# Order of quarter products and turned tiles where a row norm hands over to the next matrix product

## The reference

```python
# block 1
x = x + rmsnorm(merged @ w_out[l], norm_mix_post[l])
h = rmsnorm(x, norm_ffn_pre[l])
f = jnp.square(jax.nn.relu(h @ w_ff1[l])) @ w_ff2[l]
x = x + rmsnorm(f, norm_ffn_post[l])
# block 2
h = jnp.einsum('bsd,de->bse', x, w_in[l])
...
x = layernorm_2(DEEPNORM_ALPHA * x + mix, ln1_g[l], ln1_b[l])
hid = jax.nn.silu(x @ w_gate) * (x @ w_up)
x = layernorm_2(DEEPNORM_ALPHA * x + hid @ w_down, ln2_g[l], ln2_b[l])
# block 3
h = x @ w_in[l]
...
x = layer_norm(DEEPNORM_ALPHA_3 * x + mix, ln1_g[l], ln1_b[l])
xa = memory_cross_attention(x, mem, ...)          # begins with x @ xa_wq
x = layer_norm(DEEPNORM_ALPHA_3 * x + xa, ln2_g[l], ln2_b[l])
ff = hierarchical_moe(x, ...)
```

## Time and profile before

| what | value |
|---|---|
| median of 3 runs | 3252.77 us (3252.38 to 3253.66) |
| the profiled execution's own time | 3252.19 us |
| its span, first to last instruction | 3250.5 us |
| TensorE matmul busy | 3020.5 us, 93% of the span |
| VectorE / ScalarE / GpSimd busy | 1443.4 / 694.7 / 123.4 us (44% / 21% / 4%) |
| mean granted TensorE clock | 0.958 of full |
| last part of the span | from about 2700 us on the experts' weights stream in at some 424 GB/s with all DMA engines busy |

### The profile page before, as it was taken

How to read it: one execution, slowest core, us unless ns; L and a number is a source line. 1 busy time by engine, 2 the same in 40 slices (tenths; PEclk the granted TensorE clock), 3 DMA queues, 4 the chain that set the end, 5 groups by cost and what they waited for, 6 DMA issues and landing times. The chain is left out here.

```text
span 3250.5 us, 38522 instructions
## 1 busy us (share of the span) xinstructions
PE 3020.5 (93%) x15046; PEld 2156.2 (66%) x15046; DVE 1443.4 (44%) x2554; ACT 694.7 (21%) x1596; POOL 123.4 (4%) x147
## 2 busy tenths in 40 slices
PE   8979998999999889988999999999889977999997
PEld 4468766888868668887688886877756634333332
DVE  3454424334353667457543354424744232333335
ACT  0321113220010543471101001114531212111111
POOL 1000000000000200000100000000100001000000
PEclk9989999999999979998999999998999988999998
DMA  9121212222221102201223222222012208999995
GB/s 379 53 78 52 78 58 78 78 104 85 78 80 65 40 27 78 78 1 39 78 78 104 78 89 92 78 81 79 2 66 78 67 0 337 423 425 422 424 424 218
DMA packets 129894, 420.48 MB, mean 129 GB/s; under 512 B 6705, under 2 KB 35778, under 8 KB 108242
## 3 DMA queue, kind: packets, MB, share of 16 engines
q1 hardware_dynamic: 121842, 379.48, 30.6%
q10 hardware_dynamic: 3024, 23.59, 1.8%
q0 software_dynamic: 4880, 15.35, 1.3%
HBM read 394.81 MB, written 23.59 MB: 129 GB/s over the span
## 5 line engine op out<-in xcount | busy, mean ns | idle before, releaser
L777 PE MATMUL bank<-arena 128*128 128x256 f32 x5152 | 1127.7, 382 | 30.5 <-issue 15.5
L777 PEld LDWEIGHTS bank<-arena 128*128 128x128 f32 x5152 | 985.7, 192 | 173.1 <-issue 23.1
L1073 PE MATMUL bank<-arena 128*128 128x256 f32 x1652 | 362.7, 382 | 10.0 <-PEq L131 3.5
L1073 PEld LDWEIGHTS bank<-arena 128*128 128x128 f32 x1652 | 316.5, 192 | 54.9 <-issue 11.3
L178 PE MATMUL bank<-arena 128*128 128x512 f32 (+8 forms) x676 | 230.0, 495 | 33.1 <-PEq L3463 11.5
L178 PEld LDWEIGHTS bank<-arena 128*128 128x128 f32 (+2 forms) x676 | 120.0, 196 | 137.5 <-issue 120.3
L425 PE MATMUL bank<-arena 128*128 128x512 f32 x384 | 167.7, 598 | 4.2 <-PEq L1685 2.0
L3903 DVE TENSOR_TENSOR arena<-arena,bank 128x512 f32<-128x512 f32 x128 | 87.8, 688 | 139.0 <-PE bank L3807 136.7
L841 DVE TENSOR_TENSOR arena<-arena 128x1024 f32<-128x1024 f32 x46 | 56.3, 1223 | 182.9 <-PE bank L777 179.5
L425 PEld LDWEIGHTS bank<-arena 128*128 128x128 f32 x384 | 73.1, 191 | 95.5 <-issue 95.5
L3807 PE MATMUL bank<-arena 128*128 128x512 f32 x256 | 123.1, 615 | 4.4 <-DVE arena L3889 4.4
(11 more groups left out here) (561 smaller groups left out, 3523.9 us busy)
## 6 DMA issues: line engine op xcount, KB each, us to landing
arena<-in_moe_w_gate_dram SPq DMA_DIRECT2D x64, 1024.0 KB, 20.4
arena<-in_moe_w_up_dram SPq DMA_DIRECT2D x64, 1024.0 KB, 18.7
arena<-in_moe_w_down_dram SPq DMA_DIRECT2D x32, 2048.0 KB, 24.1
arena<-in_w_in_dram SPq DMA_DIRECT2D x29, 2048.0 KB, 7.9
arena<-in_w_ff_dram SPq DMA_DIRECT2D x16, 2048.0 KB, 7.9
x_slots<-arena ACTq DMA_DIRECT2D x8, 2048.0 KB, 33.6
arena<-in_w_out_dram SPq DMA_DIRECT2D x8, 2048.0 KB, 7.8
arena<-in_w_gate_dram SPq DMA_DIRECT2D x11, 1024.0 KB, 5.4
```

What stands on the lines that cost most here:

```text
L777: last = pe.matmul(bank[:, m, :], lhsT, rhs, start=fresh and m == 0 and k == 0, stop=k == 3, skip_group_check=True)
L1073: last = pe.matmul(bank[:, m, :], x[:, k, m * P:(m + 1) * P], w[:, k, :], start=opening and m == 0 and k == 0, stop=k == w.shape[1] - 1, s ...
```

## The change

It does four things.

- **Order on TensorE.** After product 1 of step 0, only tile 2 is turned; then comes product 2 of step 0; then tile 3 is turned; then come products 1 and 2 of step 1, and then products 5, 6, 7, 3, 4 of step 0, the same five of step 1, and the later steps as before.
- **Room for it.** Products 1 and 2 of step 1 get bank 4 (`of_12_ahead`), and the copy of its product 1 gets the first 512 columns of `spare` (`first_ahead`).
- **Copies of turned tiles.** In the layer norms ScalarE makes both copies of tiles 0 and 1, at the top of its turn for tiles 2 and 3; VectorE keeps one half of tiles 2 and 3. In handover 1 VectorE makes both copies of tile i-2 at the top of its turn for tile i. In handover 2 the copies stay as they are.
- **Copy of product 1 on ScalarE.** For step 0 it stands in the norm, ahead of the last tiles' copies (in handover 1 ahead of the squares of the last tile, L650); for step 1 it stands first in the follower's part. The waits are adapted to the new order.

The diff, cut to its changed lines with little around them:

```diff
-def products_by_tile(c, pe, keys, hidden, tail, filled, ready, turned, source, follow=None, first_turned=()):
+def products_by_tile(c, pe, keys, hidden, tail, filled, ready, turned, source, follow=None, first_turned=(), freed=()):
...
         turn_tile(i)
+        if follow and i == NT - 2:
+            follow.pe_second(pe)
     if follow:
-        follow.pe_rest(pe)
+        follow.pe_rest(pe, freed)
...
             products_by_tile(c, pe, keys, hidden, tail, filled, ready, turned, lambda i: x[:, i, :], follow,
-                             ((emptied_v, 2), (emptied, 2)))
+                             ((emptied, 4),), ((emptied_v, 1), (emptied, 5)))
...
-                if i >= 2:
-                    empty_turned(dve, i - 2, 0).then_inc(emptied_v.sem, emptied_v.up())
                 dve.wait_ge(root.sem, root.at(i + 1))
...
             if follow:
-                follow.dve(dve, ((emptied_v, NT), (emptied, NT)))
+                follow.dve(dve, ((emptied_v, 2), (emptied, 6)))
...
             for i in range(NT):
+                if i >= 2:
+                    for half in range(2):
+                        empty_turned(act, i - 2, half).then_inc(emptied.sem, emptied.up())
                 act.wait_ge(var.sem, var.at(i + 1))
...
-                if i >= 2:
-                    empty_turned(act, i - 2, 1).then_inc(emptied.sem, emptied.up())
+            if follow:
+                follow.act_first(act)
             for i in (NT - 2, NT - 1):
...
             products_by_tile(c, pe, keys, hidden, tail, filled, lambda i: (ready, ready.at(i + 1)), turned, source,
-                             follow, ((emptied_v, 4),) if again else ((emptied_v, 2), (emptied, 2)))
+                             follow, ((emptied_v, 4),) if again else ((emptied_v, 2), (emptied, 2)),
+                             ((emptied_v, 6),) if again else ((emptied_v, 3), (emptied, 3)))
...
             for i in range(NT):
+                if i >= 2 and again:
+                    for half in range(2):
+                        empty_turned(dve, i - 2, half).then_inc(emptied_v.sem, emptied_v.up())
                 dve.wait_ge(squared.sem, squared.at(2 * i + 2))
...
                 dve.tensor_tensor(x[:, i, :], x[:, i, :], work, ALU.add).then_inc(added.sem, added.up())
-                if i >= 2:
+                if i >= 2 and not again:
                     empty_turned(dve, i - 2, 0).then_inc(emptied_v.sem, emptied_v.up())
-                    if again:
-                        empty_turned(dve, i - 2, 1).then_inc(emptied_v.sem, emptied_v.up())
                 if again:
...
                 act.activation(inv[:, i:i + 1], inv[:, i:i + 1], ACT.Sqrt).then_inc(root.sem, root.up())
+                if follow and i == NT - 1:
+                    follow.act_first(act)
                 if again:
...
-    FIRST_ORDER, ORDER = (1, 2, 5, 6, 7, 3, 4), (1, 5, 6, 7, 2, 3, 4)
+    ORDER = (1, 5, 6, 7, 2, 3, 4)
+    AHEAD = ((0, 1), (0, 2), (1, 1), (1, 2)) + tuple((n, m) for n in range(2) for m in (5, 6, 7, 3, 4))
...
                       [c.region(parts[0], parts[1] + n * 512, 2, 256) for n in range(n_parts)])
-        self.of_12, self.of_6, self.of_53, self.of_74 = (
-            c.banks[n][:, :].rearrange("p (m t) -> p m t", m=2) for n in range(4))
+        self.of_12, self.of_6, self.of_53, self.of_74, self.of_12_ahead = (
+            c.banks[n][:, :].rearrange("p (m t) -> p m t", m=2) for n in range(5))
+        self.first_ahead = c.spare[:, 0:512].rearrange("p (m t) -> p m t", m=2)
         self.product, self.summed, self.combined, self.first_copied, self.fifth_copied = (c.sig(tag + n) for n in (
...
-    def products_of(self, n):
...
-        return self.FIRST_ORDER if self.follows and n == 0 else self.ORDER
+    def is_ahead(self, n):
+        return self.follows and n == 1
...
+    def sum_12(self, n):
+        return self.of_12_ahead if self.is_ahead(n) else self.of_12
...
+    def first_of(self, n):
+        return self.first_ahead if self.is_ahead(n) else self.parts[0]
...
     def done(self, n, number):
-        return self.product.at(7 * n + self.products_of(n).index(number) + 1)
...
+        at = self.AHEAD.index((n, number)) if self.follows and n < 2 else 7 * n + self.ORDER.index(number)
+        return self.product.at(at + 1)
...
             self.c.weights(pe, key)
-            if n:
+            if n and not self.is_ahead(n):
                 pe.wait_ge(self.c11_done.sem, self.c11_done.at(n))
-            self.multiply(pe, a11, b11, self.of_12, by_token, True)
+            self.multiply(pe, a11, b11, self.sum_12(n), by_token, True)
         elif number == 5:
...
             pe.wait_ge(self.first_copied.sem, self.first_copied.at(n + 1))
-            self.multiply(pe, a12, b21, self.of_12, by_token, False)
+            self.multiply(pe, a12, b21, self.sum_12(n), by_token, False)
         elif number == 3:
...
-        for number in numbers or self.products_of(n):
+        for number in numbers or self.ORDER:
             self.one(pe, n, number)
...
         key, by_token, kind, dsts = self.steps[n]
-        first, fifth, both, three = self.parts[0:4]
+        first, (fifth, both, three) = self.first_of(n), self.parts[1:4]
         c12, c21, c22 = self.parts[4:7] if kind == "gated" else dsts[1:4]
...
+    def copy_first(self, act, n):
+        act.wait_ge(self.product.sem, self.done(n, 1))
+        act.activation(self.first_of(n), self.sum_12(n), ACT.Copy).then_inc(self.first_copied.sem, self.first_copied.up())
...
         key, by_token, kind, dsts = self.steps[n]
-        first, fifth = self.parts[0:2]
-        act.wait_ge(self.product.sem, self.done(n, 1))
-        if n:
-            act.wait_ge(self.joined.sem, self.joined.at(n))
-        act.activation(first, self.of_12, ACT.Copy).then_inc(self.first_copied.sem, self.first_copied.up())
+        fifth = self.parts[1]
+        if not self.follows or n > 1:
+            if n:
+                act.wait_ge(self.joined.sem, self.joined.at(n))
+            self.copy_first(act, n)
         act.wait_ge(self.product.sem, self.done(n, 5))
...
         if kind == "copied":
-            act.activation(dsts[0], self.of_12, ACT.Copy).then_inc(self.c11_done.sem, self.c11_done.up())
+            act.activation(dsts[0], self.sum_12(n), ACT.Copy).then_inc(self.c11_done.sem, self.c11_done.up())
         elif kind == "gated":
-            act.activation(dsts[0], self.of_12, ACT.Silu).then_inc(self.c11_done.sem, self.c11_done.up())
+            act.activation(dsts[0], self.sum_12(n), ACT.Silu).then_inc(self.c11_done.sem, self.c11_done.up())
             act.wait_ge(self.c12_done.sem, self.c12_done.at(n + 1))
...
         else:
-            self.finish(act, kind, 0, dsts[0], self.of_12, self.c11_done)
+            self.finish(act, kind, 0, dsts[0], self.sum_12(n), self.c11_done)
             act.wait_ge(self.c12_done.sem, self.c12_done.at(n + 1))
...
-    def pe_rest(self, pe):
...
-        self.sevens.pe(pe, 0, Sevens.FIRST_ORDER[1:])
-        for n in range(1, len(self.sevens.steps)):
-            self.sevens.pe(pe, n)
+    def pe_second(self, pe):
+        self.sevens.one(pe, 0, 2)
...
+    def pe_rest(self, pe, freed=()):
...
+        for signal, count in freed:
+            pe.wait_ge(signal.sem, signal.at(count))
+        for number in (1, 2):
+            self.sevens.one(pe, 1, number)
+        for n in range(len(self.sevens.steps)):
+            self.sevens.pe(pe, n, (5, 6, 7, 3, 4) if n < 2 else None)
...
+    def act_first(self, act):
+        self.sevens.copy_first(act, 0)
...
+        self.sevens.copy_first(act, 1)
         for n in range(len(self.sevens.steps)):
...
-    def tiles(self, pe, filled, used, ready, turned, source, emptied_v, emptied, follow):
+    def tiles(self, pe, filled, used, ready, turned, source, copied, follow):
...
         left = (((self.joined_three, 2), (self.c11_done, 2)), ((self.c12_done, 2), (self.c21_done, 2)),
-                ((used, 2),), ((emptied_v, 1), (emptied, 1)))
+                ((used, 2),), copied(0))
...
                 turn_tile(i - 2)
-        follow.pe_first(pe, ((emptied_v, 2), (emptied, 2), (used, 3)))
-        for i in (NT - 2, NT - 1):
-            turn_tile(i)
+        follow.pe_first(pe, copied(1) + ((used, 3),))
+        turn_tile(NT - 2)
+        follow.pe_second(pe)
+        turn_tile(NT - 1)
         follow.pe_rest(pe)
...
             sevens.tiles(pe, filled, used, ready, turned, lambda i: x[:, i, :],
-                         emptied_v, emptied, follow)
+                         lambda i: ((emptied, 2 * i + 2),), follow)
...
-                if i >= 2:
-                    empty_turned(dve, i - 2, 0).then_inc(emptied_v.sem, emptied_v.up())
                 dve.wait_ge(root.sem, root.at(i + 1))
...
                 empty_turned(dve, i, 0).then_inc(emptied_v.sem, emptied_v.up())
-            follow.dve(dve, ((emptied_v, NT), (emptied, NT)))
+            follow.dve(dve, ((emptied_v, 2), (emptied, 6)))
...
             for i in range(NT):
```

(9 more changed lines are left out.)

## The result

| | before | after |
|---|---|---|
| median of five runs | 3253.66 us (3252.38 to 3254.70) | 3236.35 us (3231.19 to 3239.82) |
| the profiled execution, its span | 3252.19, 3250.5 | 3233.31, 3231.7 |
| mean granted clock | 0.958 | 0.960 |

The ratio of the times is 0.9945, interval 0.9932 to 0.9958: 17 us faster. The forecast was 3228.0, so three tenths of the expected gain are missing, and the range (to 3236.5) held it by 0.15 us.

What follows compares the result with a forecast made beforehand. TensorE, busy 93% of the span, was taken as the bound, with 24.4 us of gaps before product 1 and 9.0 of low clock. Handovers 6.03, 0.22, 5.68, 5.74, 6.67 and last norm 0.25 sum to 24.6: 3228.0 us, range 3223 to 3236.5.

Steps and rivals of the forecast that it cites:

- Part 1: Product 1 starts earlier: 2.87, 4.01 and 3.95 us at handovers 3 to 5, 5.94 at handover 1, 0 at handover 2.
- Part 2: TensorE's clock keeps its level: 2.59, 1.51 and 2.50 us back at handovers 3 to 5, 0.89 at handover 1.
- the choice that the rows left open: Whether the clock holds behind handover 1's 2.9 us gap: bounds 0 or 2.40 us lost, 1.51 taken.
- Rival B: The clock falls all the same at each handover, 6.60 + 0.89 us not won: 3235.7 us, chance 0.13.
- The rule of the Trainium skill: Frequent small idle spells between groups of matmuls can make TensorE's clock swing; by it the clock gain would be nothing.
- Part 3: Turns and waits between product 1 and product 5: 0.22 us won at handovers 2 to 5, 0.80 lost at handover 1.
- Part 4: Steps 0 and 1 have 17.4 us each instead of 24.4: cost 0, otherwise a wait up to 2 us a handover.
- rival C: In the steps of five TensorE waits for VectorE or ScalarE, up to 2 us at five places: 3238, chance 0.07.
- rival E: Step 1's weights are not there when its products come early: slower, 3277 us at 10 us each, chance 0.03.
- Part 5: In the last norm VectorE's 0.69 us copy before tile 3's reciprocal is gone: 0.25 us won, bounds 0 and 0.45.
- so the end moves with it: The 24.6 us lie in front of the router and the experts' stream begins behind it, so the gain reaches the end.
- Rival D: Nothing arrives at the end, because the experts' weights set a time of their own: 3252 us, chance 0.05.

Runs made afterwards that it cites:

- Order alone: The changed kernel's TensorE order and early copy of product 1, with copies of turned tiles as in the kernel before: 3256.9 us, ratio 0.9999.
- the copies alone: Copies of turned tiles as in the changed kernel, TensorE's order and ScalarE's copy of product 1 as in the kernel before: 3231.19 us, ratio 0.9931.
- nothing of step 1 ahead: The changed kernel, but product 5 of step 0 follows without products 1 and 2 of step 1 before it: 3249.53 us, ratio 0.9988.
- the pair with fills: Thirteen unread identity turns at the start of block 3's sparse attention, added to the kernels after and before: 3220.67 and 3252.70 us.

## Why the prediction was right, and where it was not

**Part 1, right.** Product 1 starts 1.78 us after tile 1's turns (forecast 1.89) at handovers 3 to 5, and 3.82 (3.95) at handover 1; nothing moved at handover 2. Order alone, which leaves this part out, wins nothing, and the copies alone win 20.1 of the 25.8 us.

**Part 2, right, with the choice that the rows left open.** The level held at handovers 3 to 5 (3.56 us for product 1). At handover 1 it fell behind 2.78 us; product 1 got 0.69 us back, where I took 0.89. Rival B did not come: at handovers 3 to 5 two gaps stand near each other, 0.74 and 0.69, at a clock of 1.00. The rule of the Trainium skill that I held against the change (TensorE: Matmul & The Clock Gate, "A second HAM failure mode: psum-queue depth-cycling") is not borne out there. But the margin was small: the copies alone lost the level at handover 5 behind 0.74, 1.22 and 1.27. And falls behind gaps of 0.3 to 0.9 us did come in block 3's attention, where my prediction never looked.

**Part 3, right, on the careful side.** The wait for the copy was 0.69 instead of 0.85, which makes 0.43 us at handover 2 instead of 0.22. With product 1 of step 1 in place nothing waits for t1; with nothing of step 1 ahead the wait is 2.7 us, 3.3 at handover 1. At handover 1, where I took 0.80 lost, 0.58 were. Tile 3's norm never made TensorE wait, while the copies alone left up to 1.57.

**Part 4, right.** In the page's group only 1.2 us of idle time is left beside the gaps of the handovers (11.8 less 2.78, 2.13, 3 x 0.74 and 5 x 0.69), so rival C did not come, nor a wait for a DMA (rival E). **Part 5, right:** 0.24 instead of 0.25.

By its terms the sum was 24.6 and the handovers gave 25.8. **The step that failed** is the one behind the sum: "so the end moves with it". I took all time outside of the handovers as fixed. It isn't: 7.0 us of 25.8 were given back in the profiled execution, 6.6 of them where the clock fell at other places in unchanged stages, and the median of after stood 3 us above that execution. Rival D had the sign of this (the gain does not arrive), but another cause, the experts' weights; the experts' stretch moved by 0.5 us only. The range held by luck: it reached as far as 3236.5 for the sake of rival B, which did not come, and the loss that did come happened to be of that size.

What sets whether the clock falls there stays open. Fills show that a fall at the start of the stage can be taken away; the pair with fills and the gap of 2.72 us show that records, busy time and gaps just ahead, as the profile has them, don't decide the next one. The Trainium skill (the same page, Part 1, "What's actually happening") says that the clock looks at activity in windows that run free of the program, so that one kernel can differ from run to run. The spread of one program's runs (copies alone: 3231 and 3244) and the pair with fills agree with it, and so does the gap of 2.72 us, but no run here shows those windows.

## What to carry to other kernels

Take a copy that a matmul waits for out from behind elementwise work first, and only then reorder the matmuls: here the order brought nothing alone, and 5.7 us inside the handovers once the copies were early. A gap of TensorE is paid twice if the clock falls behind it. Shorter gaps with whole products between them kept the level here (0.74 and 0.69), but three in a row of 0.74 to 1.27 once did not, so close gaps rather than split them: put independent products where the copy of one can hide behind another. A gain from a gap arrives at the end only as far as the other stages keep their clock: look for stages with TensorE half busy, compare several runs, and try a few idle turns there, for they may be worth as much as the change (here 12 to 16 us), or little (1 to 6 us in the kernel before).

## What the runs showed of the hardware

- Behind gaps of 0.69, 0.74 and 2.13 us in a row of quarter products the granted clock stayed at 2.4 GHz (1.00), each time. Inside the handovers it fell each time behind 2.70 to 3.30 us (the five gaps with nothing of step 1 ahead, and the one ahead of product 1 at handover 1 wherever the copies came early), and cost at most 1.0 to 1.7 us. In the kernel before, 3.73 to 4.86 cost 1.5 to 2.6.
- These are no limits: behind the same gap of 2.72 us between 3 and 4 it fell in twelve traces and not in two, behind 2.54 near 725 us it fell in two and not in twelve, and behind 0.74, 1.22 and 1.27 within 9 us it fell once (copies alone, handover 5).
- In a stage of short matmuls of mixed kinds it fell 2 us behind a gap of 0.63 us in one kernel and not behind 0.62 in another, with the same 223 records ahead.
- Thirteen turns that take 2.0 us, at the start of one stage, took 16.8 us off it (427.9 to 411.1) and 15.2 in the kernel after (428.1 to 412.9), and none in the kernel before (424.2 to 426.5).
- One program's runs stood up to 13 us apart (copies alone: four at 3231, two at 3243 and 3244, nothing between).
